# A hybrid decoder layer on one core: where the decay exponential, four weight splits, silu of z and the last z eviction stand in the queues

## What is computed

```
y = h @ w_in            # q,k,v of GDN | z | a | b | NSA q, kv, gates
qkv = silu(causal_depthwise_conv(qkv));  q, k = l2norm(q), l2norm(k)
g = cumsum(-exp(a_log) * softplus(a + dt_bias))     # within a chunk
decay = where(tril, exp(g_i - g_j), 0)
lower = where(strict, (k*beta) @ k.T * decay, 0);  T = inv(I + lower)
u, w = T @ (v*beta), T @ (k*beta*exp(g))
per chunk: v_new = u - w @ S;  o = (q*exp(g)) @ S + qk @ v_new
           S = S*exp(g_last) + k_dec.T @ v_new
o = rmsnorm(o) * silu(z)
x = x + concat(o, o_nsa) @ w_out
```

## Time and profile before

| | us |
|---|---|
| median of 3 runs | 1126.64 (1125.02 to 1127.02) |
| the profiled execution's own time | 1126.86 |
| its span in the trace | 1125.1 |
| PE busy in it | 1088.9 (97%) |
| DVE, ACT, POOL busy | 775.9, 449.7, 448.0 |
| mean granted TensorE clock, share of full speed | 0.987 |

### The profile page before, as it was taken

One profiled execution on the slowest core, in us unless ns is written; L12 is line 12 of the kernel. 1 busy time (PEld: TensorE's weight loads), 2 busy tenths in 40 slices (PEclk: granted clock), 3 DMA queues, 4 the chain that ended last, 5 costly groups with the idle time before them and its releaser, 6 DMA issues.

```text
span 1125.1 us, 20194 instructions
## 1 busy us (share of the span) xinstructions
PE 1088.9 (97%) x8512; PEld 943.1 (84%) x8512; DVE 775.9 (69%) x937; ACT 449.7 (40%) x632; POOL 448.0 (40%) x289
## 2 busy tenths in 40 slices
PE   6899999999999999899999999999999999999997
PEld 5799899988998888777787667888898899989986
DVE  5998479936986566543456377656997489927964
ACT  6543245413444434311223566434443144414432
POOL 0662169505823000313301289523481279307812
PEclk9999999999999999899999999999999999999998
DMA  6234233332323322113102001032233233332322
GB/s 227 75 123 150 75 111 91 134 94 96 103 85 99 107 75 76 38 58 133 39 27 63 27 2 36 22 95 77 74 112 112 82 106 112 115 110 76 103 84 75
DMA packets 34590, 98.45 MB, mean 88 GB/s; under 512 B 3664, under 2 KB 10320, under 8 KB 32848
## 3 DMA queue, kind: packets, MB, share of 16 engines
q1 hardware_dynamic: 34224, 97.26, 26.5%
q10 hardware_dynamic: 288, 0.08, 0.0%
HBM read 95.24 MB, written 2.10 MB: 87 GB/s over the span
## 4 chain that ended last, share of the span: by engine, by line
PE 86%; DVE 8%; ACT 3%; issue 2%; DMA 0%; POOL 0%; DVEq 0%; ACTq 0%
PE bank L593 24%; PE bank L594 24%; PE bank L595 24%; PE bank L2114 3%; PE bank L1900 2%; PE bank L1867 1%; PE bank L1888 1%; DVE hb_lo L717 1%; DVE w_lo L1021 1%; DVE cv L1612 1%; PE bank L2172 1%; DVE w_lo L1098 1%; PE bank L2169 1%; PE bank L1707 1%; DVE x L960 1%
## 5 line engine op out<-in xcount | busy, mean ns | idle before, releaser
L593 PE MATMUL bank<-hb_hi,w_hi 128*128 128x256 f32 x1064 | 295.9, 278 | 6.9 <-DVE w_lo L1021 3.4
L595 PE MATMUL bank<-hb_hi,w_lo 128*128 128x256 f32 x1064 | 295.0, 277 | 0.0
L594 PE MATMUL bank<-hb_lo,w_hi 128*128 128x256 f32 x1064 | 295.0, 277 | 0.0
L593 PEld LDWEIGHTS bank<-hb_hi,w_hi 128*128 128x128 f32 x1064 | 200.7, 189 | 8.9 <-DVE w_lo L1098 4.1
L595 PEld LDWEIGHTS bank<-hb_hi,w_lo 128*128 128x128 f32 x1064 | 200.7, 189 | 0.0
L594 PEld LDWEIGHTS bank<-hb_lo,w_hi 128*128 128x128 f32 x1064 | 200.6, 188 | 0.2
L593 PE MATMUL bank<-act_hi,w_hi 128*128 128x512 f32 (+1 forms) x460 | 180.3, 392 | 10.2 <-DVE w_lo L1034 9.8
L594 PE MATMUL bank<-act_lo,w_hi 128*128 128x512 f32 (+1 forms) x460 | 179.7, 391 | 0.0
L595 PE MATMUL bank<-act_hi,w_lo 128*128 128x512 f32 (+1 forms) x460 | 179.5, 390 | 0.0
L1015 ACT ACTIVATE w_hi<-raw 128x1536 fp32r<-128x1536 f32 (+1 forms) x67 | 108.8, 1623 | 161.6 <-PE bank L595 161.6
L1021 DVE TENSOR_TENSOR w_lo<-raw,w_hi 128x1536 fp32r<-128x1536 f32 (+1 forms) x67 | 159.2, 2376 | 15.9 <-ACT w_hi L1015 15.3
(11 more groups left out here) (312 smaller groups left out, 1718.2 us busy)
## 6 DMA issues: line engine op xcount, KB each, us to landing
raw<-in_gate_up SPq DMA_DIRECT2D x43, 1024.0 KB, 5.4
raw<-in_w_in SPq DMA_DIRECT2D x13, 1024.0 KB, 4.9
raw<-in_down SPq DMA_DIRECT2D x8, 1024.0 KB, 5.2
raw<-in_down SPq DMA_DIRECT2D x16, 512.0 KB, 4.3
raw<-in_down SPq DMA_DIRECT2D x8, 768.0 KB, 4.2
raw<-in_w SPq DMA_DIRECT2D x8, 512.0 KB, 4.0
x<-in_x SPq DMA_DIRECT2D x4, 512.0 KB, 7.5
raw<-in_w_out SPq DMA_DIRECT2D x4, 512.0 KB, 4.6
```

Of the source, the lines that this page charges most:

```text
L593: pe.matmul(out_ap, wh, xh, start=first, stop=False)
L594: pe.matmul(out_ap, wh, xl, start=False, stop=False)
L595: return pe.matmul(out_ap, wl, xh, start=False, stop=last)
```

## The change

Four things move, and nothing is added or left out.

1. In round 0 the addition of the decay argument (DVE) goes ahead of the walk through the schedule, directly behind `dve_projection`, so ahead of `dve_scalars_end` and the split of half 2. The exponential (ACT) goes with it: `act_scalars_end` and then the exponential now stand ahead of the three copies and the split of half 2.
2. In `act_half_end` the split of half n + 2 stands ahead of silu of z. That is so for n = 10 and n = 11, as there is no split behind n = 12 and 13.
3. `half_end` of half 13 goes ahead of round 38: DVE evicts the last z ahead of the last `state`, ACT takes its silu ahead of the last output's copy and squares.
4. PE's, POOL's and SP's queues keep their order.

```
@@ schedule()
             if n == 0 and g == len(KGROUPS) - 1:
                 out.append(("scalars",))
+            if (n, g) == (HALVES_N - 1, len(KGROUPS) - 1):
+                out.append(("half_end", n))
             if n and r < len(ROUNDS):
                 out.append(("gdn", r))
...
-        out.append(("half_end", n))
+        if n < HALVES_N - 1:
+            out.append(("half_end", n))
@@ act_half_end()
-            elif kind == "z":
+            if n + 2 < HALVES_N:
+                act_half_split(act, n + 2)
+            if kind == "z":
                 act.wait_ge(proj_evac, CONV_EVACS + n - 3)
                 act.activation(z[:, n - 10, :], z[:, n - 10, :], ACT.Silu).then_inc(z_silu, 1)
-            if n + 2 < HALVES_N:
-                act_half_split(act, n + 2)
@@ act_mixer()
             act_projection(act)
+            act_scalars_end(act)
+            act_gdn(act, 0, "g_arg")
             act.activation(ident_bf[:, :], ident, ACT.Copy).then_inc(consts_bf, 1)
...
-                if what == "scalars":
-                    act_scalars_end(act)
-                elif what == "half_end":
+                if what == "half_end":
@@ dve_mixer()
             dve_projection(dve)
+            dve_gdn(dve, 0, "g_arg")
```

More of the change, by code:

```diff
@@ L2438, in act_mixer @@
                     for tt, name in ROUNDS[n[0]]:
-                        act_gdn(act, tt, name)
+                        if (tt, name) != (0, "g_arg"):
+                            act_gdn(act, tt, name)
             act_out(act)
@@ L2465, in dve_mixer @@
                     for tt, name in ROUNDS[n[0]]:
-                        dve_gdn(dve, tt, name)
+                        if (tt, name) != (0, "g_arg"):
+                            dve_gdn(dve, tt, name)
             dve_out(dve)
```

## The result

| | us |
|---|---|
| before, median of 5 runs beside it | 1126.64 (1124.09 to 1127.02) |
| after, median of 5 runs | 1118.16 (1115.88 to 1123.60) |
| ratio, 95% interval | 0.9939 (0.9914 to 0.9964), some 6.9 us less |
| forecast | 1122.3, range 1119.8 to 1125.4 |
| the profiled execution's own time | 1123.60, the slowest of its five |

The profile alone hides this: the profiled execution is 3.3 us faster than the one of before, while the ratio says 6.9 us and the two medians 8.5. The other four executions took 1115.88 to 1118.24. The ratio's interval alone (4.1 to 9.7 us) would still hold 4.4.

A forecast was written before the change was run, and what follows sets the result against it. PE was taken as busy almost throughout, bounded by its waits and lower clock; 1.93 + 0.9 + 1.07 + 0.5 = 4.4 us off 1126.86 gave 1122.5, or 1122.2 by the median, stated as 1122.3, range 1119.8 to 1125.4.

The forecast's parts named there:

- What bounds the kernel: Whole kernel: PE is busy almost throughout, so only its waits or its time at the lower clock can give time back.
- meeting point: A weight load or attention's chain where PE's waits come back, so nothing is gained: 1126.7, chance 0.08.
- First part: Round 0, near 460 us: earlier decay argument and exponential let `lt` and PE's `k_tok` start sooner; gain 1.93 us.
- drain of 1.38 us: ACT's table load at 455: if a drain were paid only on the new chain, gain 0.55 there, time 1123.8.
- Second part: Splits ahead of silu: nothing for n = 10; for n = 11 PE's whole `vnew` wait goes, gain 1.07 us.
- Third part: Last z eviction, near 631 us: silu leaves the chain ahead of attention; gain 0.5 us, between 0.45 and 0.61.
- The clock: Behind `k_tok`, 462.20 to 467.4: half-clock work shrinks from 5.2 to 3.4 us; gain 0.9 us, the least certain term.
- Sum: Whole kernel: 1.93 + 0.9 + 1.07 + 0.5 = 4.4 us, with everything behind 651 us moving as one; 1122.3.
- the rival at 0.17: Clock gives more: no fall at 460 or a shorter one behind 641.5; 1120.6 or 1118.5, put at 1120.5; chance 0.17.
- The cap: Attention, behind 641.5: of 10.2 us at half clock POOL is busy for 6.41, so at most 3.8 us return.
- The slower rival: Between 467 and 632 us: PE, arriving earlier, is held at half clock; 1133.6 with two further stretches; chance 0.05.

The follow-up runs named there:

- third experiments: Changed kernel with DVE's `rb` and `kk` ahead of the split of half 2, ACT's copies behind it: 1118.90; also with unread matmuls in PE's waits: 1114.59.
- the change again: The whole change once more, unaltered, against the kernel before: 1119.55 (6 runs), ratio 0.9941.
- the filled kernel: Kernel before with unread matmuls in PE's waits ahead of `kq` (15), the first `k_tok` (5) and the third attention pair (8): 1120.66, ratio 0.9943.

## Why the prediction was right, and where it failed

*What bounds the kernel.* Right. What the change gave came through PE's waits and its clock; every us won at 460 was still there at 607, with no meeting point between. (The quicker stretch at 828 is neither, but doesn't go with the change.)

*First part, the chain.* Right. Forecast: exponential at 456.06, `lt` at 459.52, `k_tok` at 460.27, gain 1.93. Measured: 456.08, 459.42, 460.15, gain 2.05. The addition started 0.1 earlier than forecast, since DVE was done with its convolution before ACT's last silu. The order of lateness (POOL ahead of w_lo) was right, and the third experiments used it. The table load again took 1.28 us at 454.56, and the exponential started 0.24 behind its end with two small activations between. So the Trainium skill's drain of 1.38 us (ScalarE: Activation LUTs, "What ACT_TABLE_LOAD costs"), by which the time would have been 1123.8, isn't on this chain either.

*Second part.* Right: PE's wait for `vnew` is gone, the split for n = 10 is worth nothing by the list of waits, and the part is worth 1.11 us against 1.07 in each of the seven traces that have it.

*Third part.* Right in its mechanism: `state` was not delayed, silu was out of the chain. Size: 0.52 (forecast 0.5) in each of the seven traces that have it. The term was a choice between 0.45 and 0.61, so part of the fit is luck.

*The clock.* **This is the step that failed.** In "Sum" I closed with "Behind 651 us everything follows on PE and moves as one", and I took the stretch of 10.2 us at 641.5 as the same before and after. A shorter stretch there stood only in the rival at 0.17, with "at most 3.8 us can come back". Three things were wrong in that:

- The 10.2 us were what one execution drew. Of the eight traces without fillers in the attention five have a fall there and three have none, the changed kernel once either way; of the six with fillers none has. So its price is a chance times 4.0 to 6.5 us, a term that the sum put at nothing. The clock as a whole gave some 3 us (estimates of 2.5 to 3.3), where the sum had 0.9 for the first place, and the traces gave that place just 0.9 at best. That the change lowers the chance of the fall in the attention is the likely reading, not a shown one.
- The cap was too low: the 10.2 us less POOL's 6.41 gave 3.8, but the distance between fixed instructions gives 4.0 for the same 10.2 us, and up to 6.5 for longer falls. So the rival's 1118.5, so near the measured 1118.16, is close by luck: it is the whole of one such fall, on top of the sum, in every execution.
- The range's lower end (1119.8) took in only the clock term at 460 (1120.6) and a little more. With 3.3 in place of 0.9 the forecast would have been 1126.9 - 3.5 - 3.3 = 1120.1; the first median lies another 2 us below, which its few executions allow (the six of the change again have 1119.55).

For the place at 460 alone the 0.9 was fair: the stretches are 3.4, 3.4 and 6.8 us in the three unfilled traces with the first part as it is, and the clock there gave back 0.9, 0.9 and -0.3 us.

*The slower rival* fell: full clock from 466 to 606 and from 607 to 627 in after's trace. Three traces, the change again among them, do have one more stretch between 817 and 830, in the last feed-forward step, well behind the place named.

**What stays open.** Which part of the change makes the fall in the attention rarer isn't settled, nor strictly that it is rarer: the traced executions of the splits alone and of the eviction alone have no fall, that of the first part alone has one, but there is one trace of each, the ratios of the first two can't be told from 1, and none of the three has a mean granted clock above 0.9890, where the whole change has 0.9910. Nor is it settled how often it falls in either kernel, and with some 3 us either way on the 3.3 the share that the attention has of it is argued, from the 3.0 us that its filler brings in the kernel before against 1.6 at the first place, and not measured. Why some traces are 1 us quicker at 828 is open too.

## What to carry to other kernels

Where a profile shows a stretch at the lower clock behind a short wait, don't take its length as given for the next kernel: price it as there or not there, by the distance between two fixed instructions around it, and let the range hold both. Such distances also resolve a wait of 0.5 us that the times of whole executions don't. When few executions were taken, see where the profiled one stands among them before reading a gain from a pair of profiles. To tell clock from waits, fill the waits in both kernels with matmuls that nobody reads; where they are no longer than the wait and the clock falls there, they are an improvement as well.

## What the runs showed of the hardware that was not expected

- Matmuls that nobody reads pay: 28 of them in the kernel before, 7.0 us of PE's time, gave 0.9943 (6.3 us).
- They can narrow the spread, but needn't: on one chip 18 runs of the kernel before lay between 1122.77 and 1127.22, and five of the filled one with the splits moved within 0.21 us; the six of the filled kernel before spread over 3.3 us on theirs.
- The clock also fell with no wait in front: in before's trace for 3.4 us from 392.3, behind 16 one-column matmuls that took 1.95 us; it did so in eight of the fourteen traces, at 1.55 us each. And in after's trace it fell in the attention behind waits of no more than 1.7 us, among many short matmuls.
- At full clock the same 238 matmuls took 28.0 us in one trace and 27.0 in another.
- The lengths of all falls read inside the kernel were 3.4, 6.8, 10.2, 13.7 and 17.1 us.
